# Where the pieces of a conditioning product are placed in the order of a mixer

## The reference, cut to what matters

```python
def step(state, inp):
    r_t, w_t, k_t, v_t, a_t, b_t = inp
    sa = jnp.einsum('bhij,bhj->bhi', state, a_t)
    state = (state * w_t[:, :, None, :] + sa[..., None] * b_t[:, :, None, :]
             + v_t[..., None] * k_t[:, :, None, :])
    return state, jnp.einsum('bhij,bhj->bhi', state, r_t)
```

```python
mod = jax.nn.silu(c) @ w_mod[l] + b_mod[l]
mod_c = jax.nn.silu(c_ctx) @ w_mod[l] + b_mod[l]
```

## Time and profile before

| | |
|---|---|
| median of 3 runs | 3644.76 us (3640.76 to 3646.14) |
| the profiled execution's own time | 3640.39 us |
| its span, first to last instruction | 3638.6 us |
| mean granted TensorE clock | 0.967 of full |
| TensorE busy | 3394.2 us, 93% |
| VectorE busy | 2817.3 us, 77% |
| ScalarE busy | 1527.8 us, 42% |
| GpSimd busy | 709.6 us, 20% |
| DMA moved | 799.39 MB, mean 220 GB/s |

### The profile page before, as it was taken

One profiled execution on the slowest core, in us unless ns is written; L12 is line 12 of the kernel. 1 busy time (PEld: TensorE's weight loads), 2 busy tenths in 40 slices (PEclk: granted clock), 3 DMA queues, 4 the chain that ended last, 5 costly groups with the idle time before them and its releaser, 6 DMA issues.

```text
span 3638.6 us, 53214 instructions
## 1 busy us (share of the span) xinstructions
PE 3394.2 (93%) x21102; PEld 2856.1 (78%) x21102; DVE 2817.3 (77%) x3273; ACT 1527.8 (42%) x2091; POOL 709.6 (20%) x461
## 2 busy tenths in 40 slices
PE   8997999999997899999788999999799789999996
PEld 8995789999995799997555777777686677777775
DVE  8876667888876677876758888888574688888884
ACT  1013132100013132011334888888431358888883
POOL 0000230100000130100001443443100024433430
PEclk9998999999998999999999999999899999999998
DMA  6545243555544344551035999999642269999993
GB/s 236 188 170 199 93 148 142 186 186 186 186 167 185 111 157 151 186 185 70 1 116 185 378 377 371 371 371 379 273 186 104 82 241 346 352 355 342 348 348 133
DMA packets 119853, 799.39 MB, mean 220 GB/s; under 512 B 33824, under 2 KB 35872, under 8 KB 49440
## 3 DMA queue, kind: packets, MB, share of 16 engines
q1 hardware_dynamic: 78480, 735.14, 54.2%
q0 software_dynamic: 39024, 59.61, 4.6%
q10 hardware_dynamic: 2080, 1.05, 0.1%
HBM read 808.77 MB, written 71.83 MB: 242 GB/s over the span
## 4 chain that ended last, share of the span: by engine, by line
PE 80%; DVE 14%; ACT 3%; DMA 1%; issue 1%; DVEq 0%; POOL 0%; SPq 0%; ACTq 0%; POOLq 0%
PE ps L450 76%; PE ps L464 4%; DVE ring_r L397 2%; DMA ring<-yd_dram 1%; DVE ring_r L396 1%; DVE ring_r L2778 1%; DVE arena L2222 1%; DVE ring L1251 0%; DVE arena L1164 0%; ACT arena L1716 0%; DVE arena L1402 0%; DVE mrow L2008 0%; DVE arena_r L533 0%; ACT arena_hi L2842 0%; ACT arena L1424 0%
## 5 line engine op out<-in xcount | busy, mean ns | idle before, releaser
L450 PE MATMUL ps<-arena_r,ring_r 128*128 128x256 f32 (+1 forms) x9840 | 1278.2, 288 | 35.0 <-DVE ring_r L397 15.5
L450 PEld LDWEIGHTS ps<-arena_r,ring_r 128*128 128x128 f32 x9840 | 1219.7, 189 | 72.0 <-DVE ring_r L397 15.7
L450 PE MATMUL ps<-ring_r,arena_r 128*128 128x512 f32 (+1 forms) x2906 | 806.3, 392 | 5.6 <-DVE arena_r L2094 5.2
L450 PEld LDWEIGHTS ps<-ring_r,arena_r 128*128 128x128 f32 x2906 | 528.9, 189 | 117.5 <-DVE arena_r L2094 5.6
L450 PE MATMUL ps<-arena_hi,arena_r 128*128 128x512 f32 x1540 | 507.8, 397 | 4.7 <-DVE ring_r L2803 4.7
L397 DVE TENSOR_TENSOR ring_r<-ring,ring_r 128x4096 fp32r<-128x4096 f32 (+2 forms) x104 | 445.3, 4282 | 3.6
L2919 POOL DMA_INDIRECT yd_dram<-arena,small x129 | 228.4, 1771 | 732.2 <-PE ps L464 629.3
L450 PEld LDWEIGHTS ps<-arena_hi,arena_r 128*128 128x128 f32 x1540 | 290.2, 188 | 69.4 <-DVE ring_r L2803 5.1
L2778 DVE TENSOR_TENSOR ring_r<-ring,ring_r 128x2048 fp32r<-128x2048 f32 x130 | 298.0, 2292 | 22.6 <-ACT ring_r L2842 14.9
L2778 DVE TENSOR_TENSOR ring_r<-ring,arena_hi 128x2048 fp32r<-128x2048 f32 x128 | 293.5, 2293 | 24.1 <-ACT arena_hi L2842 17.3
L396 DVE CAST ring_r<-ring 128x4096 fp32r<-128x4096 f32 (+2 forms) x104 | 256.7, 2468 | 56.5 <-PE ps L450 45.0
(11 more groups left out here) (343 smaller groups left out, 3524.7 us busy)
## 6 DMA issues: line engine op xcount, KB each, us to landing
ring<-wexp_dram SPq DMA_DIRECT2D x387, 1024.0 KB, 8.4
ring<-stream_dram SPq DMA_DIRECT2D x143, 2048.0 KB, 7.7
ring<-yd_dram SPq DMA_DIRECT2D x7, 2048.0 KB, 11.9
arena<-yd_dram SPq DMA_DIRECT2D x5, 2048.0 KB, 9.7
xd_dram<-arena POOLq DMA_DIRECT2D x6, 512.0 KB, 5.8
consts_sb<-consts_dram SPq DMA_DIRECT2D x1, 2242.0 KB, 15.9
arena<-xd_dram,small POOLq DMA_INDIRECT x129, 10.5
yd_dram<-arena,small POOLq DMA_INDIRECT x129
```

The costliest lines, as they stand in the source:

```text
L450: return pe.e.matmul(ps, lhsT=lhsT, rhs=rhs, start=start, stop=stop, skip_group_check=True)
```

## The change

Three edits in `weave`, and a name in TensorE's `piece`.

- TensorE's key-norm products get a name of their own, "key norms", and are issued right behind the first `fill(2)`. VectorE's "roots" stays where it was.
- The second `fill` in the opening becomes `fill(3)` (before: 2), the third becomes `fill(2)` (before: 3), and the `fill(5)` behind the turned tiles goes.
- Each step of the inverse is followed by `fill(1)` (before: `fill(0.75)`).

```diff
             piece("before")
             fill(2)
+            piece("key norms")
             piece("scans")
             piece("query")
             piece("exps")
             piece("identities")
             level()
-            fill(2)
+            fill(3)
             piece("keys")
             piece("roots")
             piece("hats")
-            fill(3)
+            fill(2)
             piece("hgates")
             level()
             piece("hturned")
             piece("turned")
-            fill(5)
             for g in range(3):
                 piece("first", g)
                 level()
@@
             for i in range(18):
                 piece("inverse", i)
                 level()
-                fill(0.75)
+                fill(1)
             tail()
@@
             def piece(name, i=0):
-                if name == "roots":
+                if name == "key norms":
                     for g in (0, 4):
```

## The result

| | before | after |
|---|---|---|
| median, 20 runs each | 3645.28 us (3637.72 to 3648.72) | 3650.58 us (3641.79 to 3656.80) |
| profiled execution, span | 3638.6 us | 3653.8 us |
| mean granted clock | 0.967 | 0.963 |

A forecast was written before the change was run, and what follows sets the result against it. The prediction took TensorE to bound the inverse, and pieces behind the turned tiles to stand on the path. Its terms, -12.5 + 2.0 + 8.4 + 5.0 = +2.9 us, gave 3647 us, range 3637 to 3655.

The forecast's parts named there:

- Opening, key norms: In the mixer's opening, twelve key-norm products come one products piece earlier; they were already early, so cost 0.
- The emptied place: Behind the turned tiles, pieces 7 to 11 leave the path: gain 6.5 us in layer 0, 6.0 in layer 1.
- First products: At the mixer's first products, an added fold delays group 2: +1.0 us a layer, bounds -1.1 and +1.8.
- Steps 0 to 12: In the inverse, bound by TensorE, three more products pieces and one fold cost their length: +4.2 us a layer.
- Rival B: The inverse has hidden slack and takes the added pieces for nothing: -10.5 us, 3634, faster; chance 0.12.
- Steps 13 to 17: Late inverse steps: a piece behind `attended` adds 1.89 us, another comes behind the normalisation wait; +2.5 us a layer.
- rival C: The clock falls from `attended` on in both layers, with the new piece at half speed: +11.6 us, 3656; chance 0.18.
- Tail: Last stretch of each layer: same pieces and same weight chunks behind them, nearly its old time, within 3 us.
- A: The forecast itself: pieces leave one place on the path and land on another, +3 us, 3647; chance 0.60.

The follow-up runs named there:

- only the move: Kernel before, without the five pieces behind the turned tiles and with one piece a step of the inverse; opening unchanged: 3647.29 us, ratio 1.0013.
- pieces in waits: Changed kernel with six pieces taken from the inverse and, with those of the first products, put where TensorE stands idle: 3627.48 us, ratio 0.9946 to before.
- only the opening: Changed kernel with the pieces behind the turned tiles and in the inverse put back as before: 3643.64 us, ratio 0.9997 to before.
- no piece in step 13: Changed kernel with the products and fold of step 13 moved one step ahead: 3640.54 us, ratio 0.9991 to before; second look 3640.08 us.
- all ahead: Changed kernel with all five pieces of steps 13 to 17 moved into steps 8 to 12: 3640.98 us, ratio 0.9990 to before.
- combined: Kernel with pieces in TensorE's waits, its last three pieces also re-placed: none in step 13, products in 14, products and fold before step 15's transposes: 3625.27 us, ratio 0.9939.
- the last run above: Combined kernel with products and fold between last scores and `attended`, products in step 12, none in steps 13 to 15: 3630.15 us, ratio 0.9960 to before.

## Why the prediction was right, and which term was mis-sized

The range and the sign of the sum held; the median is 3.6 us above the number given, and of the change +2.9 was predicted where the ratio says +6.9 (4.7 to 9.1). The terms below are measured in one profile of each kernel.

- *Opening, key norms*: 0 predicted; the run with the opening alone agrees.
- *The emptied place*: -6.5 and -6.0 predicted, -6.5 and -6.0 measured. Nothing else was late: the first products start as the transposes end (330.88).
- *First products*: +1.0 a layer predicted; -1.0 in layer 0 and +0.6 in layer 1. In layer 0 the clock was up when the piece came (341.04 to 342.02 for F), the lower bound that I had named; in layer 1 it was half (1.80 us for F, 1154.92 to 1156.72).
- *Steps 0 to 12*: +4.2 a layer predicted, +4.5 and +3.5 measured. Rival B, hidden slack in the inverse, is refuted. The Trainium skill (Perfetto Trace Analysis, Identifying the Most-Contended Engine) judges TensorE's headroom by the work done against the peak and by the busy share of weight loads. By that share the pieces would have found room. This trace does not agree: it was 19.03 of 22 us, and yet steps took pieces at full length.
- *Steps 13 to 17*: +2.5 a layer predicted, +3.9 and +9.4 measured from `attended` to the tail. This is the term that was mis-sized. I priced the new piece at full clock, 1.89; it took 3.55. I took layer 1's full clock as what would stay. From `attended` to the second product was to grow by 1.9 us; it grew by 3.0 in layer 0 and 5.3 in layer 1. The drop, rival C with 0.18, came in both layers of both profiles of the changed kernel.
- *Tail*: 0 predicted within 3 us; +0.5 and +1.3 measured.

These terms add up to some +10 us, near rival C's +11.6 and far from A's +2.9. So the condition that A rested on, full clock in layer 1, did not hold in the profiles, and that the median lies nearer to A's number than to C's 3656 is in part luck. One reason shows in the times: the profiled execution of the changed kernel took 3655.55 us, and its 20 executions span 3641.79 to 3656.80 at mean clocks of 0.967 to 0.962. The two profiles have 0.963 and 0.962, the low end, so that the drop comes in both layers of every execution is not shown.

How often does it come? Over all profiles, by layers: with pieces right behind `attended` (changed kernel twice, only the move, pieces in waits) 8 of 8. With nothing behind and 1.45 us idle in front (before, only the opening, no piece in step 13 twice, all ahead, combined) 6 of 12. With a piece in the idle and none behind 1 of 8. The drop begins before the piece behind `attended` runs, so what lies in front may be the better division: 14 of 20 layers with 1.45 us idle there, 1 of 8 with 0.49 or less. These are few layers, two to an execution. Even so, the forecast should have been a mean over the drop and not one layer of each.

What stays open is the cause of the drop. That one piece moved from behind `attended` into the idle in front of it takes some 12 to 15 us off is shown. That the idle is what brings the clock down is not: it fell once without any, and it begins within 3 us of the start of `attended`, before the piece behind it runs. The moved piece changed both, and no run left the idle out while it kept a piece behind.

## What to carry to other kernels

When work leaves a place on the path, ask for the bound of the place where it lands. Where steps differ by exactly the length of their filler, that engine is the bound and filler is paid in full. Taken out, it pays back only until the next engine is the bound: with it gone from some steps, TensorE stood idle there for 0.66 us. Filler belongs in that engine's waits for others, counted at the lower clock: there were some 4.8, 5.6, 2.8 and 1.5 us of them a layer here, and using them made the kernel 0.6% faster than before, where spreading the pieces evenly made it 0.2% slower.

## What the runs showed of the hardware that I had not expected

In 15 of 28 layers the granted clock went to the 1.2 GHz level for some 7 to 14 us in the middle of busy TensorE work. In 11 of them TensorE had worked for 60 us or more without a gap of 0.3 us, up to the 1.45 us idle; in the other four two gaps of 0.67 us lay in that stretch, and in one of these (layer 1 of the last run above) there was no idle in the 25 us ahead. The Trainium skill (TensorE: Matmul & The Clock Gate, Part 1) has activity release the clock and idling lose it; that run does not agree. All 15 came within 3 us behind the start of the first `attended` product; why there was not tried.
